# TensorE's order over the token tiles: mixing a tile ahead of pooling the next

## The reference

```python
def pool_mixer(h, w_grp, scale):            # h = rms_norm(x, norm_mix)
    hg = h.reshape(bsz, s, 4, 256)          # 4 groups, windows 2, 4, 8, 16
    csum = jnp.cumsum(hg, axis=1)
    for g, win in enumerate((2, 4, 8, 16)):
        c = csum[:, :, g]
        outs.append((c - lagged_by(win)) / count - hg[:, :, g])
    y = jnp.einsum("bsgc,gcd->bsgd", pooled, w_grp).reshape(bsz, s, d)
    return y * scale
...
x = x + pool_mixer(rms_norm(x, norm_mix), pool_w, pool_scale)
x = x + hier_moe(rms_norm(x, norm_ffn), ...)   # top-1 of 4 groups, top-2 of its 8 experts
return rms_norm(x, norm_final)
```

## Time and profile before

| | |
|---|---|
| median of 3 runs | 704.4 us (704.3 to 706.5) |
| the profiled execution | 705.32 us, span 703.5 us |
| TensorE busy | 669.0 us, 95% of the span |
| VectorE, ScalarE, GpSimd busy | 605.8, 528.6, 246.5 us |
| HBM traffic | 368 GB/s over the span |
| granted TensorE clock, mean | 0.978 |

### The profile page before, as it was taken

How to read it: one execution, slowest core, us unless ns; L and a number is a source line. 1 busy time by engine, 2 the same in 40 slices (tenths; PEclk the granted TensorE clock), 3 DMA queues, 4 the chain that set the end, 5 groups by cost and what they waited for, 6 DMA issues and landing times.

```text
span 703.5 us, 10781 instructions
## 1 busy us (share of the span) xinstructions
PE 669.0 (95%) x3678; PEld 565.2 (80%) x3678; DVE 605.8 (86%) x465; ACT 528.6 (75%) x441; POOL 246.5 (35%) x198
## 2 busy tenths in 40 slices
PE   7799989999999999999999999999999999999870
PEld 5799978888888888888888888888888888888660
DVE  6787698889999999999999999999999999999773
ACT  6797626878777777777777777777778887777772
POOL 3000012144444444444444444444444445412410
PEclk9999989999999999999999999999999999999995
DMA  8997768999999999999999999999999999980294
GB/s 314 417 407 246 272 270 308 360 362 381 384 381 381 380 377 381 383 380 385 369 385 383 378 393 385 375 397 358 407 387 383 374 387 383 385 311 11 28 345 169
DMA packets 44858, 242.01 MB, mean 344 GB/s; under 512 B 9552, under 2 KB 10712, under 8 KB 20258
## 3 DMA queue, kind: packets, MB, share of 16 engines
q1 hardware_dynamic: 34322, 220.39, 80.0%
q0 software_dynamic: 10512, 21.30, 11.4%
HBM read 229.29 MB, written 29.36 MB: 368 GB/s over the span
## 4 chain that ended last, share of the span: by engine, by line
PE 92%; DVE 4%; ACT 2%; DMA 1%; issue 1%; POOLq 0%; SPq 0%; ACTq 0%; DVEq 0%
PE psum L1390 75%; PE psum L1410 4%; PE psum L1319 3%; PE psum L1305 2%; PE psum L1421 2%; PE psum L1337 2%; DVE raw L1270 1%; PE psum L1345 1%; PE psum L1328 1%; PE psum L1284 1%; DMA nm_rows<-in_norm_mix 0%; PE psum L1379 0%; DMA out<-raw 0%; DVE xs L911 0%; DVE pt_lo L916 0%
## 5 line engine op out<-in xcount | busy, mean ns | idle before, releaser
L985 DVE TENSOR_TENSOR w_lo<-raw,w_hi 128x2048 fp32r<-128x2048 f32 (+1 forms) x193 | 437.1, 2280 | 50.0 <-ACT w_hi L733 49.5
L733 ACT ACTIVATE w_hi<-raw 128x2048 fp32r<-128x2048 f32 x191 | 362.3, 1915 | 38.7 <-PE psum L1390 38.7
L1390 PE MATMUL psum<-w_hi,x_hi 128*128 128x512 f32 x512 | 162.5, 398 | 0.0
L1390 PE MATMUL psum<-w_lo,x_hi 128*128 128x512 f32 x512 | 158.7, 391 | 0.0
L1390 PE MATMUL psum<-w_hi,x_lo 128*128 128x512 f32 x512 | 158.2, 390 | 0.0
L595 POOL DMA_INDIRECT total<-ysb,dst_now x30 | 56.4, 1879 | 235.7 <-ACT ysb L808 235.7
L1390 PEld LDWEIGHTS psum<-w_hi,x_lo 128*128 128x128 f32 x512 | 96.1, 188 | 21.1
L1390 PEld LDWEIGHTS psum<-w_lo,x_hi 128*128 128x128 f32 x512 | 96.1, 188 | 20.9
L1390 PEld LDWEIGHTS psum<-w_hi,x_hi 128*128 128x128 f32 x512 | 91.4, 188 | 21.4 <-DVE w_lo L985 5.4
L1390 PE MATMUL psum<-w_hi,h_hi 128*128 128x512 f32 x256 | 82.6, 404 | 1.9 <-ACT ysb L808 1.8
L1390 PE MATMUL psum<-w_lo,h_hi 128*128 128x512 f32 x256 | 80.2, 395 | 0.0
(11 more groups left out here) (154 smaller groups left out, 655.2 us busy)
## 6 DMA issues: line engine op xcount, KB each, us to landing
raw<-in_expert_w_gu SPq DMA_DIRECT2D x128, 1024.0 KB, 8.0
raw<-in_expert_w_down SPq DMA_DIRECT2D x64, 1024.0 KB, 7.1
res<-in_x SPq DMA_DIRECT2D x8, 512.0 KB, 9.7
normed<-nx POOLq DMA_DIRECT2D x8, 512.0 KB, 6.3
total<-res SPq DMA_DIRECT2D x8, 512.0 KB, 8.0
raw<-total SPq DMA_DIRECT2D x8, 512.0 KB, 7.8
out<-raw SPq DMA_DIRECT2D x8, 512.0 KB, 3.5
pw_in<-in_pool_w SPq DMA_DIRECT2D x1, 1024.0 KB, 8.7
```

The lines of the kernel that those rows point to most:

```text
L733: nc.scalar.activation(w_hi[:, r, :], raw[q][:], ACT.Copy).then_inc(hi_done, 1)
L985: return V.tensor_tensor(w_lo[q][:, c0:c1], raw[q][:, c0:c1], w_hi[:, r, c0:c1].bitcast(f32), ALU.subtract)
L1390: last = mm(dst[:, n * N:(n + 1) * N], a[:, ch, :], b[:, c * D + n * N:c * D + (n + 1) * N], start=(ch == 0 and a is hi and b is b_hi), st ...
```

## The change

On TensorE, from step 1 on, a tile is mixed ahead of the pooling of the next tile; the transposes stay first and the logits last. In step 1, seven identity matmuls stand between the transposes of tile 0 and the mixing of tile 1. On VectorE, in step 0, the low part of the pooled tile 1 is made ahead of the third bf16 part of tile 2; the other steps keep their order.

```diff
@@ VectorE
                 if i >= 1:
                     norm_2(i - 1)
+                if i == 0:
+                    pooled_low(1)
                 if i + 2 < TILES:
                     split_rest(i + 2)
-                if i + 1 < TILES:
+                if 1 <= i < TILES - 1:
                     pooled_low(i + 1)
                 if i + 3 < TILES:
                     scale_x(i + 3)
@@ TensorE
             for i in range(TILES):
                 if i >= 1:
                     turn_tile(i - 1)
-                else:
+                if i == 1:
+                    keep_warm(7, LG)
+                if i >= 0:
                     mix_tile(i)
                 if i + 1 < TILES:
                     pool_tile(i + 1)
-                if i >= 1:
-                    mix_tile(i)
                 if i >= 1:
                     logits_tile(i - 1)
             turn_tile(TILES - 1)
```

## The result

The changed kernel takes 724.8 us (median of 4 runs, 724.7 to 726.05), the kernel before 704.54 us over four (704.3 to 706.5). The ratio is 1.0287, 95% interval 1.0275 to 1.0299: 20.3 us slower. Forecast were 720.3 us and a range of 713.0 to 724.5, so the sign and the new waits came as forecast, the clock cost more than forecast, and the time lies 0.3 us above the range.

A forecast was written before the change was run, and what follows sets the result against it. TensorE, with 92% of the chain that ended last, was taken as the bound. 704.4 plus 10.1 us (10.97 of new waits less 0.85 at the start) plus 5.8 for the clock gave 720.3 us, range 713.0 to 724.5.

The forecast's parts named there:

- A shift of the tile part reaches the end: Between tiles and expert part: a microsecond lost or won among the tiles is a microsecond of the kernel.
- VectorE, tile 1's lower part first: VectorE, step 0: lower part starts about 25.67, ends 26.89; tile 3's reciprocal and ScalarE's queue move 0.94 us earlier.
- The identity matmuls: TensorE, step 1: seven matmuls, under 1 us, inside the wait for tile 1's lower part, costed at nothing.
- Tile 1: TensorE's start: mixing of tile 1 at 27.03, its transposes at 36.41, 0.85 us before the present 37.26.
- The other tiles: Tiles 2 to 6: transposes wait for VectorE's addition behind the next split; periods 9.88 and 9.58 us, 10.97 us lost.
- The clock: TensorE behind the six new waits: granted clock falls at four of six, 1.46 us each, 5.8 us in all.
- The second clock row: Profile window 95.50 to 102.40, clock 0.51: taken to show about 2 us of waiting within 4 us can cause a fall.
- the 1.46: Price of one clock fall in us: pooling plus mixing at 29.12 to 35.48, 6.36, against 4.90 at 2.4 GHz.
- The rival in which the clock holds: Tile loop: new waits without clock falls, 704.4 + 10.1 = 714.5 us, up to 716 with one fall; chance 0.29.

The follow-up runs named there:

- dve_only: The kernel before with only the VectorE part of the change, TensorE's order as before; 705.01 us, ratio 0.9993.
- no_warm7: The changed kernel without the seven identity matmuls of step 1; 726.06 us, ratio 1.0299.
- add_first_no_warm: The `add_first` kernel without the seven identity matmuls; 702.16 us, ratio 0.9965.
- add_first: The changed kernel with, on VectorE from step 1 on, the addition of mixed tile i ahead of the lower part of pooled tile i+1; 702.17 us, ratio 0.9964.
- fill8: The changed kernel with eight identity matmuls behind the logits of steps 1 to 6, inside TensorE's waits; 713.73 us, ratio 1.0132.
- add_first_old_pe: The `add_first` kernel with TensorE in the old order, pooling ahead of mixing, and no identity matmuls; 703.88 us, ratio 0.9988.
- pe_only: The kernel before with only the TensorE part of the change, VectorE's order as before; 727.33 us, ratio 1.0320.
- add_first_low_late: The `add_first` kernel with tile 1's lower part again behind tile 2's third part on VectorE; 703.91 us, ratio 0.9990.
- step1_only: The changed kernel with TensorE's old order, pooling ahead of mixing, from step 2 on; 704.72 us, ratio 1.0006.
- fill14: The changed kernel with 14 identity matmuls behind the logits of steps 1 to 6; 721.1 us, ratio 1.0231.

## Why the forecast was right in kind and short in size

- **A shift of the tile part reaches the end.** Right: what follows the tiles has kept its length to 0.03 us (the two windows of 618.8).
- **VectorE, tile 1's lower part first.** Right. It starts 0.03 behind ScalarE's upper part, and third part and reciprocal follow in steps of 1.14. `dve_only` shows the 0.95.
- **The identity matmuls.** Wrongly sized: fourteen instructions, 1.5 us to the next start, not under 1. Still inside the wait (mixing at 26.30), so the cost of nothing stands, as `no_warm7` and `add_first_no_warm` show.
- **Tile 1.** 11.88 us from the transposes of tile 0 instead of 12.83: 0.95 won, forecast 0.85.
- **The other tiles.** Right: place, releaser and queue are those named, and `add_first` shows that it is the queue position of the addition. With the clock held, `fill8` has 83.90 - 35.73 = 48.17 us for the five periods, forecast 48.80; the sum was 0.6 long. From tile 0 to tile 7 the waits cost 65.69 - 56.19 = 9.5 us, forecast 10.1. That the profile gives the waits as 1.99 and 1.70, not 2.32 and 2.02, is in part the way they are counted, from the modelled end of the logits.
- **The clock.** This is the step that failed: "I take four falls of six: 5.8 us". There were six falls of six, and against the same stretches of `fill8` they cost 1.59, 1.36, 2.49, 1.53, 1.26 and 2.53 us, 1.8 each and not 1.46. From tile 0 to tile 7 that is 76.37 - 65.69 = 10.7 us in place of 5.8. Both factors were low, the count more than the price. The one price was that of a short fall; two of the six lasted about twice as long and cost 2.5. The second clock row had shown such a long one, with a mean of 0.51 over 6.90 us, and I took it for the question whether the clock falls, not for the question how long. The other error, 0.6 us too much for the waits, hid a little of this one. Six falls at 1.46 would have given 723.3, so my upper end left too little for unequal prices.
- **What the 1.46 was worth.** It was read from a stretch whose loss was hidden by ScalarE and VectorE, as `dve_only` showed. In the changed kernel there is no such cover: behind each wait everything is on TensorE's path until the next one. As a price of TensorE's own stretch it was a fair one for the four short falls, 1.26 to 1.59.
- **The rival in which the clock holds**, at 714.5 us, is the right price of the change without the clock: `fill8` gives 713.7. The Trainium skill's rule on idle gaps ("TensorE: Matmul & The Clock Gate", section "Why this matters for your kernels"), which stood beside it, doesn't agree with these traces: all six waits, 1.6 to 2.0 us, are shorter than the gaps that it warns of, and the clock fell with each of them. The measurement decides.

What stays open: why the clock fell with every wait of 1.6 to 2.0 us before the transposes, but not behind 2.51 us before a pooling (`dve_only`, `add_first_old_pe`) nor behind 1.9 us before a mixing (`pe_only`, `add_first_low_late`). In the first the wait stands between logits and transposes, in the others between transposes or identity matmuls and dense pooling and mixing. It doesn't take a repeated wait: `step1_only` has a single one of 1.62 us before transposes, and the clock fell with it. That the kind of work around the wait matters is a guess; no run changed it alone. Open too is why a fall lasted under 4 us in one place and nearly 7 in another.

## What to carry to other kernels

When one engine's order is changed, look for the instruction on every other engine that stands between the two results whose order was exchanged: here the addition stayed behind the split, and became the last thing that was waited for. Exchanging these two as well was worth over 22 us. Where a new wait of this size (here 1.6 to 2.0 us) comes once in every tile, cost it twice, once for itself and once at full count for the clock. Take the price of a fall from more than one fall of the old trace, and ask of each whether it was on the path there.

## What the runs showed of the hardware

- Six waits of 1.6 to 2.0 us, one in each 11 us, cost the clock each time, 1.3 to 1.6 us where it stayed low for under 4 us and 2.5 where it stayed low for nearly 7. Filling nearly all of each wait with identity matmuls kept it at 1.00 and took 11 us off the kernel.
- With 0.9 us of each filled, five waits of 0.65 to 1.02 us passed and one of 0.73 was followed by a fall. The runs spread over 4 us, where the fully filled ones agree within 0.3.
- A float32 matmul of 128 columns is two TensorE instructions in the profile and takes 0.23 us (`fill14`: 28 instructions from 44.62 to the next start at 47.83), while the transposes of the same shape are one each, 0.12 us (eight from 44.85 to 45.80 in the earlier trace rows).
